# Twelve of 36 column units of a projection computed with Strassen's seven products instead of eight

## The reference, cut to what matters

```
h = rmsnorm(h_res, norm_w[l]) * (1.0 + scale[:, None, :]) + shift[:, None, :]
proj = h @ w_in + b_in          # h: 2048 x 1024, w_in: 1024 x 4624
(na_q, na_k, na_v, na_z, ml_q, ml_k, ml_v, ml_o, ml_z, i_f, f_f, i_b, f_b) = jnp.split(proj, split_idx, axis=-1)
na_out = neighbourhood_attention(na_q, na_k, na_v, rpb) * jax.nn.silu(na_z)
qk = jax.nn.silu(centred_short_conv(jnp.concatenate([ml_q, ml_k], axis=-1), conv_w, conv_b))
# mLSTM: a recurrence over chunks of keys and values, forwards and backwards
C_new = decay[..., None, None] * C + jnp.einsum('bhs,bhse,bhsd->bhed', w, v_c, k_c)
hm = (h_fwd + h_bwd) * jax.nn.sigmoid(ml_o);  ml_out = layernorm(hm) * ml_norm_w * jax.nn.silu(ml_z)
```

## Time and profile before

| | |
|---|---|
| Runs (3) | 1885.74, 1885.39, 1884.79 us; median 1885.39 us |
| Profiled execution | span 1883.3 us from its first to its last instruction; its own time is not given, the median lies 2.1 us above the span |
| PE | 1865.6 us busy, 99% of the span |
| DVE, ACT, POOL | 52%, 33%, 29% |
| Transfers | 303.55 MB, mean 161 GB/s |
| The projection | PE from 598.3 to 1442.3 us |

### The profile page before, as it was taken

The page is one execution under the profiler, slowest core; times in us unless marked ns, Lnnn a source line. Parts: engine busy times, 40 slices in busy tenths (PEclk is TensorE's granted clock), DMA queues, the critical chain, the costliest instruction groups (busy, mean ns, idle before and its releaser), DMA issues.

```text
span 1883.3 us, 26698 instructions
## 1 busy us (share of the span) xinstructions
PE 1865.6 (99%) x10035; PEld 1540.4 (82%) x10035; DVE 982.4 (52%) x2117; ACT 618.3 (33%) x1317; POOL 552.5 (29%) x925
## 2 busy tenths in 40 slices
PE   9999999999999999999999999999999999999998
PEld 8888878888888888888888787888887777788886
DVE  6556565775666433114777322223213777776665
ACT  7321111233444432101222202221114667655552
POOL 2112222233642222110110000222314777544442
PEclk9999999999999999999999999999999999999999
DMA  6223142366897745312221123665563776867663
GB/s 197 95 79 119 62 128 81 104 184 235 306 266 252 235 168 162 101 50 84 74 78 68 53 62 116 211 211 171 168 220 105 243 232 224 271 219 241 230 229 112
DMA packets 236365, 303.55 MB, mean 161 GB/s; under 512 B 41414, under 2 KB 161126, under 8 KB 236204
## 3 DMA queue, kind: packets, MB, share of 16 engines
q1 hardware_dynamic: 205724, 215.84, 37.4%
q0 software_dynamic: 23600, 77.61, 11.4%
q10 hardware_dynamic: 6912, 8.39, 1.2%
HBM read 194.71 MB, written 107.54 MB: 160 GB/s over the span
## 4 chain that ended last, share of the span: by engine, by line
PE 94%; DVE 2%; DMA 2%; issue 1%; ACT 1%; POOL 0%; SPq 0%; POOLq 0%; DVEq 0%; ACTq 0%
PE banks L145 25%; PE banks L147 25%; PE banks L146 25%; PE banks L2106 3%; PE banks L2069 3%; PE banks L2088 3%; PE banks L2704 2%; PE banks L2706 1%; PE banks L2397 1%; DMA iraw<-in_w_in 1%; PE banks L2089 1%; PE banks L2674 1%; PE banks L234 1%; PE banks L1109 1%; PE banks L1741 0%
## 5 line engine op out<-in xcount | busy, mean ns | idle before, releaser
L145 PE MATMUL banks<-hT,wu 128*128 128x512 f32 (+1 forms) x528 | 204.6, 387 | 1.1 <-DVE wu L512 0.6
L147 PE MATMUL banks<-hT,wu 128*128 128x512 f32 (+1 forms) x528 | 202.3, 383 | 0.0
L146 PE MATMUL banks<-hT,wu 128*128 128x512 f32 (+1 forms) x528 | 202.2, 383 | 0.0
L145 PE MATMUL banks<-iT,wub 128*128 128x512 f32 x384 | 151.2, 394 | 0.0
L145 PE MATMUL banks<-iT,wua 128*128 128x512 f32 x384 | 150.8, 393 | 0.0
L145 PE MATMUL banks<-wub,iT 128*128 128x512 f32 x384 | 150.6, 392 | 0.0
L147 PE MATMUL banks<-iT,wub 128*128 128x512 f32 x384 | 149.7, 390 | 0.0
L147 PE MATMUL banks<-iT,wua 128*128 128x512 f32 x384 | 149.5, 389 | 0.0
L146 PE MATMUL banks<-wub,iT 128*128 128x512 f32 x384 | 149.5, 389 | 0.0
L147 PE MATMUL banks<-wub,iT 128*128 128x512 f32 x384 | 149.5, 389 | 0.0
L146 PE MATMUL banks<-iT,wua 128*128 128x512 f32 x384 | 149.5, 389 | 0.0
(11 more groups left out here) (293 smaller groups left out, 4116.3 us busy)
## 6 DMA issues: line engine op xcount, KB each, us to landing
iraw<-in_w_in SPq DMA_DIRECT2D x36, 512.0 KB, 4.4
wa<-in_w_ada SPq DMA_DIRECT2D x48, 256.0 KB
yT<-sg POOLq DMA_DIRECT2D x32, 256.0 KB, 3.1
oraw<-yT SPq DMA_DIRECT2D x32, 256.0 KB, 4.8
xr<-in_x SPq DMA_DIRECT2D x16, 512.0 KB, 4.4
h<-h POOLq DMA_DIRECT2D x16, 512.0 KB, 4.3
hT<-tr POOLq DMA_DIRECT2D x16, 512.0 KB, 5.1
tws<-wg SPq DMA_DIRECT2D x16, 512.0 KB, 5.1
```

The lines of the kernel that those rows point to most:

```text
L145: e.matmul(ps, lh, rh, start=first, stop=False)
L146: e.matmul(ps, lh, rl, start=False, stop=False)
L147: return e.matmul(ps, ll, rh, start=False, stop=last)
```

## The change

The parts nq, nk and mz (12 units) leave the list `work`, which then has 96 tiles and the 4 gate tiles, in the order nz, mk, mq, gates between, mv, one unit of mq, nv, one unit of mq, mo. The 12 units are computed behind it by a new class `Fast` as three pairs of double units, for each half of the tokens. Each (double unit, half) is a 2x2 block product done by Strassen's rule: 7 products of 12 matmuls where the direct way has 8. That is 6 x 14 = 84 *products* of 12 matmuls in place of 48 tiles of 24.

The products need sums and differences of quarters of the tokens and of the weights. Those that are sums are made in memory: SP copies one operand to `wsum` or `hsum` (512 KB or 1 MB), and POOL issues a transfer that adds the other onto it, 17 of each, one per list position from 21 and 26 on. Differences, high parts and low parts are made on DVE and ACT. Outputs that need several products are combined on ACT and DVE (`part`). The gates' chain and the recurrence move ahead in the list: the chain now begins in mv (from where the tiles rotate over five banks), the recurrence runs under nv, mq's last unit and mo. In list positions the new order is: 0 to 23 nz, one mk unit and the gates, 24 to 43 mk and mq, 44 to 59 mv, 60 to 63 mq, 64 to 79 nv, 80 to 83 mq, 84 to 99 mo. SP's part of it stands before the nv stores of the same position. Attention's first work is hung on products 72 to 83. The engines' queues get one more branch (the program is emitted in three pieces instead of two).

```diff
-BLOCKS = [("nq", 0), ("nk", 1), ("mv", 6), ("mk", 5), ("mq", 4), ("nv", 2), ("nz", 3), ("mz", 8), ("mo", 7)]
+PLAN = [("nz", 0), ("nz", 1), ("nz", 2), ("nz", 3), ("mk", 0), ("mk", 1), ("mk", 2), ("mq", 0), ("mq", 1), ("mk", 3),
+        ("mv", 0), ("mv", 1), ("mv", 2), ("mv", 3), ("mq", 2), ("nv", 0), ("nv", 1), ("nv", 2), ("nv", 3), ("mq", 3),
+        ("mo", 0), ("mo", 1), ("mo", 2), ("mo", 3)]
@@ Proj.sp
+            fast.copy(e, w, n)
+            states.sp(e, w, n)
             if name == "nv":
...
             for x in range(*self.after[n]):
                 self.load(e, w, x)
-            states.sp(e, w, n)
             if name == "mo":
-                att.early_sp(e, w, m)
+                fast.early_sp(e, w, m)
@@ Proj.pool
             out.tail_pool(e, w, n)
+            fast.add(e, w, n)
             states.pool(e, w, n)
@@ States
-        self.g0 = proj.nv0 + 3
-        self.s0 = proj.nv0 + 21
+        self.g0 = proj.g0 + 1
+        self.s0 = self.g0 + 18
@@ Fast
+    SEQ = [(i, q) for i, q in ((5, 0), (5, 1), (2, 0), (2, 1), (1, 0), (3, 0), (1, 1), (3, 1), (4, 0), (4, 1), (6, 0), (6, 1), (7, 0), (7, 1))]
+    DOUBLES = [(("nq", 0), ("nk", 0)), (("nq", 2), ("nk", 2)), (("mz", 0), ("mz", 2))]
+    ORDER = [(0, 0), (0, 1), (0, 2), (1, 2), (1, 0), (1, 1)]
+    def copy(self, e, w, n):
+        n -= 21
+        if 0 <= n < self.SUMS:
+            w.wait_ge(*self.proj.full.ge(n + 21))
+            if n >= 3:
+                w.wait_ge(*self.copy_in[n % 3].ge(n // 3))
+            dst, src, _ = self.sums(n)
+            e.dma_start(dst, src).then_inc(*self.copy_in[n % 3].inc())
+    def add(self, e, w, n):
+        n -= 26
+        if 0 <= n < self.SUMS:
+            w.wait_ge(*self.copy_in[n % 3].ge(n // 3 + 1))
+            dst, _, src = self.sums(n)
+            e.dma_start(dst, src, accum_op=ALU.add).then_inc(*self.added.inc())
+    def early_dve(self, e, w, m):
+        if m == 10:
+            self.tokens_difference(e, w, 0)
+        if m in self.early_x:
+            self.tokens_low(e, w, *self.early_x[m])
+        if m == 14:
+            for j in range(4):
+                self.weights_low(e, w, j)
+    def pe(self, e, att):
+        for j in range(self.N):
+            n, p = divmod(j, 14)
+            i, q = self.SEQ[p]
+            if j == self.N - 1:
+                att.first_pe(e, w)
...
+            elif i == 1:
...
+                    w.wait_ge(*self.w_out.ge(4 * n + (3 if q else 0)))
...
+            w.wait_ge(*self.t_lo.ge(j + 1))
+            w.wait_ge(*self.x_lo.ge(self.x_at[(self.ORDER[n][0], i)] + 1))
...
+            for c in range(KT // 2):
+                e.matmul(ps, t[:, 0, c], x[:, 0, c], start=new and c == 0, stop=False, skip_group_check=not new)
+                e.matmul(ps, t[:, 0, c], x[:, 1, c], start=False, stop=False, skip_group_check=not new)
+                m = e.matmul(ps, t[:, 1, c], x[:, 0, c], start=False, stop=c == KT // 2 - 1, skip_group_check=not new)
@@ Attention.act and .dve
+                if q == 0:
+                    self.fast.stored(w, self.fast.OUTS - 1)
                 w.wait_ge(*self.pt_full.ge(n + 1))
```

More of the change, by code:

```diff
@@ L1287, in __init__ @@
         self.rawn = {n: i for i, n in enumerate(n for n, j in enumerate(jobs) if j[0] != "gates" and n not in self.passing)}
[L1288 to L1296, removed]
+        self.stage, self.convs = {}, {}
         for n, (name, u, tb) in enumerate(work):
@@ L1300, in __init__ @@
             else:
[L1301 to L1309, removed]
+                self.stage[n] = len(self.stage)
+        self.users = {i: n for n, i in self.stage.items()}
+        self.evac_at, self.row_at, c = {}, {}, 0
         for n, (name, u, tb) in enumerate(work):
-            c += {"nq": 4, "nk": 1, "nz": 1, "mz": 1, "gates": 1, "mo": 1}.get(name, 0)
+            c += name in ("nz", "gates", "mo")
             self.evac_at[n] = c
@@ L1314, in __init__ @@
                 self.row_at[n] = len(self.row_at) + 1
[L1315 to L1316 removed]
         self.mo0 = next(n for n, x in enumerate(work) if x[0] == "mo")
[L1319 to L1321 removed]
+        self.g0 = g0 = next(n for n, x in enumerate(work) if x[0] == "mv")
+        self.place = [n % 8 if n < g0 else (g0 + (n - g0) % 5) % 8 for n in range(len(work))]
+        a, b, c = ((g0 + i) % 8 for i in (5, 6, 7))
+        self.reserved = [a, b, c]
     def pg(self, n):
@@ L1888, in early_sp @@
                     self.load(e, w, 0, j)
+            fast.stored(w, 40)
+            for j in self.jobs:
+                if j[0] == "q" and j[2] >= 2:
+                    self.load(e, w, 0, j)
+        if m == 78:
+            proj.stored_all(w, "nz")
+            proj.stored_all(w, "nv")
+            w.wait_ge(*fast.full.ge(m))
+            for x in range(2):
+                for j in self.jobs:
+                    if j[0] == "vz"[x]:
+                        self.load(e, w, 0, j)
+                if x == 0:
+                    self.values(e, w, 0)
+                    self.values(e, w, 1)
     def sp(self, e, w, tail):
         proj, states = self.proj, self.states
-        w.wait_ge(*proj.full.ge(len(proj.work)))
+        w.wait_ge(*self.fast.full.ge(self.fast.N))
         for i in range(2):
             w.wait_ge(*proj.ca_st[i].ge(16))
-        for name in ("mv", "mz", "mo"):
+        for name in ("mv", "mo"):
             proj.stored_all(w, name)
-        w.wait_ge(*proj.row_step.ge(48))
+        self.fast.stored(w, self.fast.OUTS)
+        self.fast.read(w)
         states.stored_all(w)
@@ L2995, in whole @@
         mixer = Mixer(k, hT, banks, norm)
+        over = [x for x in k.used[first:] if x not in (mixer.full, mixer.y_step)]
         out = FirstOut(k, banks, mixer, ident, mhalf)
         gw = GatedWeights(k, out)
-        ended = k.used[first:]
+        ended = [x for x in k.used[first:] if x not in over]
         proj = Proj(k, banks, out, gw)
         states = States(k, proj, ident)
-        att = Attention(k, proj, states, ident)
         with k.nc.Block() as block:
```

664 lines of the change are left out of this document (509 added, 155 removed).

## The result

| | |
|---|---|
| After, 4 runs | 1917.79 to 1923.02 us, median 1920.17 |
| Before, same chip | 1884.79 to 1887.79 us, median 1885.57 |
| After / before | 1.0181, 95% interval 1.0167 to 1.0196: slower |
| Profiled execution | span 1921.2 us, before 1883.3 |

A forecast was written before the change was run, and what follows sets the result against it. PE was taken to bound the kernel, busy 1865.6 of 1883.3 us. −32.7 − 1.8 + 3.6 + 1.3 + 12.5 + 1.05 + 2.5 + 1.5 = −12.0 took 1885.4 to 1873.4 us, range 1858 to 1889.

The forecast's parts named there:

- T: Adding transfers in POOL's queue: us per MB on top of 1.8, taken as 5.2 to 8, costing nothing.
- rival C: Adding transfers hold the `ca` stores, PE stops in positions 41 to 49: 1885 to 1897 us; chance 0.16.
- Term 8: Clock: after term 5's wait PE restarts at the lower level, between 0 and 5.4 us, taken as +1.5.
- Costed at nothing: Places given no time: the extra branch, the list's start, nv stores, SP's copies, DVE in the products.
- Term 1: Matmuls removed: 48 tiles of 24 become 84 products of 12, 144 fewer, −32.7 us.
- Term 5: Behind nv (position 79): PE waits at position 81 for `swv`, behind low parts and a convolution, +12.5 us.
- Term 3: Behind mv (position 59): PE waits for a small copy behind late low parts and a convolution, +3.6 us.
- Term 4: At the first nv tile (64): `swv` stands behind the store of tile 63's convolved result, +1.3 us.
- Term 6: First product: sigmoid, high and low parts in mo's positions 14 and 15 end late, +1.05 us.
- Term 7: Attention's start: four small idle spells of PE, 3.3 us against 0.78 before, +2.5 us.
- B: Rival: the wait at position 81 isn't there, 1859.4 us; chance 0.17.
- D: Rival: the products don't keep their pace because DVE or loads come late, 1879 or 1887 us; chance 0.12.

The follow-up runs named there:

- The last run: The run at 1871.63 with DVE's and ACT's first work for attention one product earlier, ahead of combining output 46: 1872.36 us, 0.9927 of before.
- the run at 1871.63: Changed kernel with halved adding transfers, mask in parts, loads apart, splits spread but earlier, recurrence first only in mq's last two units: 1871.63 us, 0.9926 of before.

## Why the prediction was wrong

**The step that failed most** is "I take T between 5.2 and 8, nothing to pay, because the plain transfer is the nearest row". An adding 1 MB took 13.7 us to land in this place and an adding 512 KB, whose pieces are narrow columns of the weights, 15.5. And the threshold was worked out for the wrong loop. The forecast asked when the queue's throughput falls behind and put the point at T = 8.1, with a lag of 21.5 us that the banks allow (a number it gives no working for). What bound was the latency: one landing and one convolution over two `ca` buffers, which is behind as soon as a store lands in more than about 6 us (2 × 5.44 − 4.9). The lag then met not the banks first but the low parts that mv needs. That the adding transfers made the 16.6 us of idle time is shown by the run with one row, where it is gone, and borne out by those with plain copies and with halves; that the loop over two buffers is what failed rests on the landings and on DVE's waits. This is rival C in its mechanism, which had a chance of 0.16; its price (11.7 to 24 us) covers the 21.6 that the run with one row gave back. In its terms the measured T was 13.7 − 1.8 = 11.9, for which its formula gives 23 us; that this comes near is partly luck, since PE stopped for the low parts and not for full banks.

**The clock.** Term 8 took 1.5 us, for the one wait of 12.5. The rows show 22.9: nearly every spell from 2.38 us on was followed by matmuls at 1.2 GHz, and attention's start held that level for some 24 us. In the first half of that stretch small waits followed each other; behind the last one, at 1479.42, PE worked without a wait and the windows to 1490 still read 0.50, and why isn't shown. The mechanism was right and its size off by 21, the largest single error of the sum; a part of it comes with the spells that the other failed steps made. The Trainium skill ("TensorE: Matmul & The Clock Gate", section "HAM oscillation — how this bites in real kernels") says that waits of a few us for transfers, between bursts of matmuls, put the engine back to the half rate each time; the trace agrees at six places and at attention's start, and differs at one: behind the 3.21 us at 1169.62 the clock stayed at 1.00.

**Costed at nothing, and wrong**: the products' first loads in mo, 3.21 + 3.55 us. The forecast listed SP's nv stores and copies but never walked mo's positions 2 and 3, where 4 MB go into the queue that carries the recurrence, and 7, where 3 MB do. Shown by the run with the loads apart.

**Terms that held.** Term 1: 144 matmuls, 2.72 us a product. Term 5: 12.5 forecast, 12.53 measured, for the weighing as named. Term 3: 3.6 and 3.78. Term 4: 1.3 (its own working, 7.0 − 5.44 − 0.46, gives 1.1), measured 2.38. Term 6: 1.05, measured 0.79, but for another reason (no row of the products' parts was waited for; the profile shows it as issue, and it may be the branch). Term 7 did not hold in size: +2.5, measured 7.54 − 0.78 = +6.8; four spells were there as forecast, the first one longer. The last run points at DVE's place behind an output that waited for its buffer: put ahead of it, this spell shrank and the next one grew.

The sum: the forecast's −12.0 against +37.9 leaves 49.9: 16.6 for the adding transfers, 21.4 for the clock, 6.8 in mo, 4.3 at attention, about 0.8 over the smaller terms. **The rivals**: B (no wait at 81) is refuted by 12.53, D by the pitch of 2.72. C gave the sign, but not alone: with the adding transfers reduced to a row, the kernel was still slower than before by 12 us: the waits behind mv and nv that I had forecast, those in mo and at attention's start that I had not or only in part, and the clock.

**That the change can pay** the run at 1871.63 shows, by 14 us. Which of its edits is needed was not tried one by one.

## What to carry to other kernels

A transfer with others behind it has to be priced by its landing, against the loop that waits for it (landing plus work, divided by the number of buffers), and by what it does to loads in other queues. Cutting it in two and spreading the halves over twice the positions gave back all that removing it did. And a wait of PE is priced with what follows it at half rate: here 51.1 us of idle cost 22.9 more, so several spells of 3 us are worth more work than their sum. When one queue's order is changed, follow the chain through the other queues (row add, store, load) before calling it a gain.

## What the runs showed of the hardware

- Adding in memory took half as long again as copying the same, or more: at the median 13.7 against 9.0 us for 1 MB, 15.5 against 9.5 for 512 KB of narrow pieces. These hold for their place in the queue: with the adding transfers in nv they were 13.2 and 10.8.
- Stores behind an adding transfer in POOL's queue landed 0.7 to 0.8 us after it, not before (three in a row from 832.40 on).
- In nv adding transfers held up loads of 256 KB in SP's queue so that PE waited up to 10.22 us.
- Idle time alone doesn't decide the clock. Behind the spell of 2.38 us at 983 the window reads 0.81, behind that of 3.21 at 1169.62 it stays 1.00. What makes the difference isn't shown.
- Behind the wait of 13.07 us the matmuls of 512 columns started 0.43 us apart, and 0.23 apart from 853.78 on, 6.1 us after the restart:

```profile
848.23 0.63 PE L146 MATMUL banks<-wub,iT 128*128 128x512 f32 x1
848.66 0.63 PE L147 MATMUL banks<-wub,iT 128*128 128x512 f32 x1
...
853.78 0.41 PE L147 MATMUL banks<-wub,iT 128*128 128x512 f32 x1
854.02 0.39 PE L145 MATMUL banks<-wub,iT 128*128 128x512 f32 x1
```
